# Two gather stages entered by token tile: head 0 of tile 0 is multiplied and searched before tile 1 is turned

## The reference, cut to what matters

```python
q = (ht @ w_query).reshape(T, Hh, 2, PEER_HALF).astype(jnp.float32)   # 8 heads, 2 halves of 128
scores = jnp.einsum('thpd,hpkd->thpk', q, sub_keys)                   # 128 keys per half
s_top, i_top = lax.top_k(scores, K)                                   # K = 16
cand = (s_top[:, :, 0, :, None] + s_top[:, :, 1, None, :]).reshape(T, Hh, K * K)
best, pos = lax.top_k(cand, K)
expert_idx = jnp.take_along_axis(cand_idx, pos, axis=-1)
gates = jax.nn.softmax(best, axis=-1)
...
u = expert_u[idx]
a = jax.nn.gelu(jnp.einsum('tkd,td->tk', u, xb)) * g
return jnp.einsum('tk,tkd->td', a, expert_v[idx])
```

## Time and profile before

| | us |
|---|---|
| median of 3 runs | 2307.51 |
| lowest and highest run | 2303.17, 2310.67 |
| profiled execution, span from first to last instruction | 2302.8 |
| profiled execution, whole time | not given by the page |
| TensorE busy | 1980.1 |
| VectorE busy | 1564.0 |
| ScalarE busy | 1017.4 |
| GpSimd busy | 612.8 |

### The profile page before, as it was taken

How to read it: one execution, slowest core, us unless ns; L and a number is a source line. 1 busy time by engine, 2 the same in 40 slices (tenths; PEclk the granted TensorE clock), 3 DMA queues, 4 the chain that set the end, 5 groups by cost and what they waited for, 6 DMA issues and landing times. The chain is left out here.

```text
span 2302.8 us, 23800 instructions
## 1 busy us (share of the span) xinstructions
PE 1980.1 (86%) x8004; PEld 1232.2 (54%) x8004; DVE 1564.0 (68%) x2910; ACT 1017.4 (44%) x2140; POOL 612.8 (27%) x561
## 2 busy tenths in 40 slices
PE   4999889777877788799978988888888878889998
PEld 3986665222322233379867534433433325878987
DVE  7977776766667676578876677666777654465654
ACT  3344344544444444435444454444454434444443
POOL 0000034443444434100003344344444440220000
PEclk9999899999999999999999999999999999999999
DMA  8786599999999999796667999999999995333553
GB/s 312 281 326 217 187 366 421 421 421 421 421 422 417 422 421 418 319 340 225 231 235 284 421 421 422 420 421 421 418 401 422 421 421 200 115 137 130 183 192 137
DMA packets 112571, 761.74 MB, mean 331 GB/s; under 512 B 12864, under 2 KB 13648, under 8 KB 26304
## 3 DMA queue, kind: packets, MB, share of 16 engines
q0 software_dynamic: 76656, 549.47, 57.6%
q1 hardware_dynamic: 34832, 207.73, 24.3%
q10 hardware_dynamic: 960, 3.01, 0.4%
HBM read 759.12 MB, written 1.05 MB: 330 GB/s over the span
## 5 line engine op out<-in xcount | busy, mean ns | idle before, releaser
L907 PE MATMUL pair<-uv,p_diag 128*128 128x512 f32 x1536 | 761.5, 631 | 190.7 <-ACT p_diag L2117 189.9
L1523 DVE CUSTOM_DVE_ANT_0 uv<-uv,p_h 128x1024 f32<-128x1024 f32 x384 | 470.3, 1225 | 336.8 <-DMA uv<-in_peer_uv,p_idx 336.3
L525 POOL DMA_INDIRECT uv<-in_peer_uv,p_idx x384 | 433.1, 1128 | 737.4 <-PE pair L907 590.0
L907 PEld LDWEIGHTS pair<-uv,p_diag 128*128 128x128 f32 x1536 | 279.1, 195 | 647.9 <-ACT p_diag L2117 391.9
L1172 DVE TENSOR_TENSOR ring_low<-ring,ring_high 128x2048 fp32r<-128x2048 f32 x148 | 336.7, 2287 | 120.3 <-ACT ring_high L1925 119.3
L2111 ACT ACTIVATE p_act<-p_dot 128x1 f32<-128x1 f32 x512 | 103.5, 202 | 652.0 <-DVE p_dot L1523 649.8
L1925 ACT ACTIVATE ring_high<-ring 128x2048 fp32r<-128x2048 f32 x148 | 279.5, 1908 | 182.4 <-DMA ring<-in_ret_w_in 45.5
L672 PE MATMUL pair<-hT_high,ring_high 128*128 128x256 f32 x992 | 287.6, 290 | 3.9 <-DVE hT_low L1182 1.5
L672 PE MATMUL pair<-hT_low,ring_high 128*128 128x256 f32 x992 | 281.9, 284 | 0.0
L672 PE MATMUL pair<-hT_high,ring_low 128*128 128x256 f32 x992 | 281.8, 284 | 0.0
L907 PE MATMUL pair<-uv_high,p_diag 128*128 128x512 f32 x512 | 246.9, 615 | 37.2 <-ACT p_diag L2117 37.1
(11 more groups left out here) (353 smaller groups left out, 2316.6 us busy)
## 6 DMA issues: line engine op xcount, KB each, us to landing
ada<-in_ada_w SPq DMA_DIRECT2D x50, 512.0 KB, 5.8
ring<-in_ret_w_in SPq DMA_DIRECT2D x24, 1024.0 KB, 5.1
ring<-in_sgu_w_in SPq DMA_DIRECT2D x24, 1024.0 KB, 8.1
ring<-in_peer_w_query SPq DMA_DIRECT2D x16, 1024.0 KB, 4.9
ring<-in_w_up SPq DMA_DIRECT2D x16, 1024.0 KB, 4.8
ring<-in_w_down SPq DMA_DIRECT2D x16, 1024.0 KB, 4.8
mod<-in_ada_w SPq DMA_DIRECT2D x30, 512.0 KB, 6.0
ring<-in_sgu_w_out SPq DMA_DIRECT2D x12, 1024.0 KB, 5.4
```

Of the source, the lines that this page charges most:

```text
L525: nc.gpsimd.indirect_dma_start(uv_rows[SLOT[l][s]].rearrange("p a d -> p (a d)"), None, experts, bass.IndirectOffsetOnAxis(ap=p_idx[:, k:k ...
L907: mm = nc.tensor.matmul(acc[:, half, :], p_diag[:, n % DIAGS, :], v[:, half * 512:(half + 1) * 512], start=(k == 0), stop=(k == PICKS - 1))
L1523: V.tensor_tensor_reduce(out=u, in0=u, in1=p_h[:, s // PICKS, :], scale=1.0, scalar=0.0, op0=ALU.mult, op1=ALU.add, accum_out=p_dot[:, n % ...
```

## The change

In both expert layers:

- TensorE turns tile 0 and multiplies head 0 for tile 0 alone (`head_columns(0, (0,))`: 48 matmuls of 128 columns), makes its scores, and only then turns tile 1. Then it multiplies head 1 for both tiles and its scores, and after these head 0 for tile 1 (48 matmuls of 128 columns), with which q0 and q1 become free, and its scores. Head 0 of the chunk has three score groups in place of two.
- Query chunk 1 is no longer multiplied ahead of the picks. Half chunks now stand ahead of picks 0, 2, 8, 14, 20 and 26, scores ahead of 4, 18 and 32. The splits of blocks q4 to q7 and the copies by ScalarE move with them. Blocks q2 and q3 use the two lower places of the high ring too, so pick 5 waits no longer for chunk 1.
- The row of modulation 7 is multiplied ahead of pick 36 (first layer).
- VectorE makes the low half of q0 ahead of tile 0's `finish_tile`, and that of q1 and tile 0's hT lows behind it. Tile 1's hT lows stand behind step 2 of the first search. Lows of q2 and q3 follow the search.
- In the second layer the norm of the memory rows moves from ahead of the picks to pick 22.
- PSUM pairs are numbered by a second order, `PAIR`.

```diff
+QUERY_AT = (0, 2, 8, 14, 20, 26)
+SCORES_AT = (4, 18, 32)
...
+def pairs_in_order():
+
+    out = list(sums_in_order())
+    for l in range(2):
+        i = out.index(("query", l, 0))
+        q0, q1, q2, q3, tile0, tile1, then = out[i:i + 7]
+        out[i:i + 7] = [q0, q1, tile0, q2, q3, then, tile1]
+    return numbered(out)
...
-        out += hT[:2] + (mods(7) if l == 0 else []) + hT[2:]
-        out += [("scores", l, c, t) for c in range(4) for t in range(TT)]
+        out += hT[:2] + [("scores", l, 0, 0)] + hT[2:] + [("scores", l, 0, 1), ("scores", l, 0, 2)]
+        out += [("scores", l, c, t) for c in range(1, 4) for t in range(TT)]
...
-    paired = {i for l in range(2) for i in range(query_first[l] + 4, query_first[l] + 10)} | set(range(kv_first, kv_first + 10))
+    paired = {i for l in range(2) for i in range(query_first[l] + 2, query_first[l] + 10)} | set(range(kv_first, kv_first + 10))
...
                     if s == 5:
-                        pool.wait_ge(sum_ready, SUM[("query", l, 1)] + 1)
+                        pool.wait_ge(sum_ready, SUM[("ret_out" if l == 0 else "sgu_out", 1)] + 1)
...
# TensorE, peer
-                head_product(l, 0)
-                head_scores(l, 0)
-                head_product(l, 1)
-                head_scores(l, 1)
-                columns_product(("query", l, 1), ("query", l), 1, hT)
-                scores(1)
+                turn_rows(n, p_h, (0,))
+                open_sum(("query", l, 0))
+                head_columns(0, (0,)).then_inc(head_ready, 1)
+                pe.wait_ge(keys_in, 16 * (l + 1))
+                pe.wait_ge(head_taken, 2 * l + 1)
+                head_scores(0, 0, (0,))
+                turn_rows(n, p_h, (1,))
+                head_columns(1, (0, 1)).then_inc(head_ready, 1)
+                pe.wait_ge(head_taken, 2 * l + 2)
+                head_scores(1, 1, (0, 1))
+                head_columns(0, (1,), taken=True).then_inc(sum_ready, 1)
+                pe.wait_ge(*taken_sum(("query", l, 0)))
+                head_scores(2, 0, (1,))
...
-                    if s in (2, 10, 18, 26):
-                        part = (2, 10, 18, 26).index(s)
-                        c = 2 + part // 2
+                    if s in QUERY_AT:
+                        part = QUERY_AT.index(s)
+                        c = 1 + part // 2
                         columns_product(("query", l, c), ("query", l), c, hT, parts=(part % 2,))
-                    if s in (16, 32):
-                        scores(1 + s // 16)
-                    if l == 1 and s == 36:
-                        sum_mod(11)
+                    if s in SCORES_AT:
+                        scores(1 + SCORES_AT.index(s))
+                    if s == 36:
+                        sum_mod(7 if l == 0 else 11)
...
# VectorE, finish_tile and last_product_and_norm
-                if n in (1, 3) and t == 1:
-                    lows_hT(n, ((0, 0), (0, 1)))
...
+                    if t == 0:
+                        lows(query_first[n // 2])
                     finish_tile(n, t, h, shift)
-                    lows(query_first[n // 2] + t)
+                    if t == 0:
+                        lows(query_first[n // 2] + 1)
+                        lows_hT(n, ((0, 0), (0, 1)))
...
# VectorE, peer
-                lows_hT(n, ((1, 0), (1, 1)))
                 first = query_first[l]
-                lows(first + 3)
                 for step in range(STEPS):
                     choose(l, 0, step)
+                    if step == 2:
+                        lows_hT(n, ((1, 0), (1, 1)))
                 if l == 1:
-                    norm(6, m_h, m_h, m_row_gain)
-                lows(first + 4)
+                    dve.wait_ge(mem_in, 16)
+                    dve.sem_inc(x_ready, TT)
+                lows(first + 3)
...
-                        if s in (3, 9, 17):
-                            lows(first + 5 + (3, 9, 17).index(s))
+                        if s in (5, 7, 11, 17):
+                            lows(first + 4 + (5, 7, 11, 17).index(s))
+                        if l == 1 and s == 22:
+                            norm(6, m_h, m_h, m_row_gain, begun=True)
...
# ScalarE, peer
+                act.wait_ge(head_ready, 2 * l + 1)
+                take_head(0, (0,), (head_taken, 2 * l + 1))
+                take_head_scores(0, 0, (0,))
+                take_hT(n, ((1, 0), (1, 1)))
+                act.wait_ge(head_ready, 2 * l + 2)
+                take_head(1, (0, 1), (head_taken, 2 * l + 2))
+                take_head_scores(1, 1, (0, 1))
+                exponentials(0)
+                act.wait_ge(sum_ready, SUM[("query", l, 0)] + 1)
+                take_head(0, (1,), taken_sum(("query", l, 0)))
                 highs(first + 3)
...
+                take_head_scores(2, 0, (1,))
                 if l == 1:
                     norm_root(6, m_h)
-                highs(first + 4)
-                take_query(1)
-                take_scores(1)
...
-                        if s in (2, 8, 14):
-                            highs(first + 5 + s // 6)
-                        if s in (13, 29):
-                            take_query(2 + s // 29)
-                        if s in (18, 34):
-                            take_scores(2 + s // 34)
+                        if s in (4, 6, 10, 16):
+                            highs(first + 4 + (4, 6, 10, 16).index(s))
+                        if s in (3, 17, 29):
+                            take_query(1 + (3, 17, 29).index(s))
+                        if s in (5, 20, 34):
+                            take_scores(1 + (5, 20, 34).index(s))
```

More of the change, by code:

```diff
@@ L191, in two_blocks @@
     SUM = sums_in_order()
+    PAIR = pairs_in_order()
     SMALL = small_in_order()
@@ L402, in sum_of @@
         def sum_of(name):
-            return pair[SUM[name] % 3]
+            return pair[PAIR[name] % 3]
         def small_of(name):
             return small[SMALL[name] % 2]
-        kv_pair = (SUM[("peer", 1, 1)] + 1) % 3
+        kv_pair = PAIR[("query", 1, 3)] % 3
         landed = {}
@@ L827, in head_product, with head_scores @@
                                 for j, (a, b) in enumerate(((high, hT[0]), (high, hT[1]), (low, hT[0]))):
[L828 removed]
+                                    mm = nc.tensor.matmul(sum_of(("query", l, 0))[:, head, nt % 2 * S + lo:nt % 2 * S + hi], a[:, k, n_tile], b[:, kk, lo:hi],
                                                           start=(kk == 0 and nt % 2 == 0 and j == 0), stop=(kk == KD - 1 and j == 2),
                                                           skip_group_check=True)
[L831 removed]
+                        if taken and kb == 0:
                             mm.then_inc(w_used, 1)
[L833 to L839 removed]
+                    return mm
+                def head_scores(part_of_chunk, head, tiles):
+                    name = ("scores", l, 0, part_of_chunk)
                     open_small(name)
[L841 to L842 removed]
+                    for q in range(2 * len(tiles)):
+                        t, part = tiles[q // 2], q % 2
                         mm = nc.tensor.matmul(small_of(name)[:, q * P:(q + 1) * P], p_qT[:, 0, 2 * head + part, t * P:(t + 1) * P],
@@ L917, in memory_block @@
                     wait_hT(6)
-                    last = max(i for i in SUM.values() if i < SUM[("peer", 1, 0)] and i % 3 == kv_pair)
-                    pe.wait_ge(sum_taken[kv_pair], last // 3 + 1)
+                    pe.wait_ge(*taken_sum(("query", 1, 3)))
                 if c and kb == 0:
@@ L1466, in choose @@
                 if step == 0:
-                    dve.wait_ge(*taken_small(("scores", l, h // 2, t if h > 1 else h)))
+                    dve.wait_ge(*taken_small(("scores", l, h // 2, t if h > 1 else 1 if h else 2 * t)))
                     for p in range(2):
```

54 lines of the change are left out of this document (16 added, 38 removed).

## The result

The changed kernel takes 2318.0 us (median of 4 runs, 2315.28 to 2318.79), the kernel before 2305.3 in the same session: a ratio of 1.0049, 95% interval 1.0035 to 1.0062. Forecast was 2303.0 with a range of 2297 to 2319, so the time lies inside the range, and the direction was wrong: 0.5% slower where 0.2% faster was forecast. (The forecast was counted from 2307.5, the median of the three runs of before that it had; the same step of 4.5 us from 2305.3 would be 2300.8.) The profiled execution took 2315.28 us with a span of 2313.5.

A forecast was written before the change was run, and what follows sets the result against it. Each gather stage was taken as bound by its bytes at about 421 GB/s. Gains of 4.3 and 1.7 us less 1.4 for holes took 4.6 off a 2302.8 span; with 4.7 between span and median, 2303.0, range 2297 to 2319.

The forecast's parts named there:

- Head 0, tile 0: First stage's entry: 48 matmuls of 128 columns at 0.111 us each; the search starts at 275.8, 9.9 us earlier.
- rival (a): Head 0's narrow matmuls cost as fp32, 0.222 us each, in both stages; total 2320, chance 0.17.
- 5.3 us, from 268.6: First stage: time and start of head 0's 48 narrow matmuls for tile 0, taken at 0.111 us each.
- The clock in the second stage: Second entry: the clock falls to half as before, costing head 0 1.75 us; the search starts at 1210.2.
- Comes back after some 3.5 us of work: Second entry: the fallen clock is full again after some 3.5 us of TensorE work, half of it, 1.75 us, lost.
- Rival (b): The clock falls in the new gaps before head 1 too, both stages, adding 4.5 us to the chain; 2312, chance 0.15.
- The rest of the entry: First stage, search to first gather: index ready at 290.6, 6.6 us earlier; q4 issued at 288.8, 0.85 us later.
- the wait for exp: Entry: VectorE's wait for exp, which stands behind head 1's copy, grows from 1.6 to about 3.6 us.
- The holes: Between the picks, TensorE's cover of the stream is gone: a hole of 0.7 us per stage, bounds 0 and 3.
- 88 against 87: Picks 2 through 32: TensorE has 88 us of work, the stream 87 us of gathers and ring blocks.
- The sum: Whole kernel: gains of 4.3 and 1.7 us less 1.4 for two holes, 4.6 us off, giving 2303.0.

The follow-up runs named there:

- fill: The changed kernel with three fp32 matmuls of 512 columns added on TensorE in its pause ahead of head 0; 2302.5 us, ratio 0.9991.
- exp_first: The changed kernel with the exp put ahead of head 1's copy in ScalarE's queue; 2319.2 us, ratio 1.0064.
- fill_exp: fill with the exp put ahead of head 1's copy in ScalarE's queue, products not spread; 2303.7 us, ratio 0.9993.
- wide: The changed kernel with head 0 of tile 0 multiplied over all 256 columns instead of 128; 2306.5 us, ratio 1.0007.

## Why the prediction was wrong

*Head 0, tile 0: right at one clock, wrong at the other.* 0.111 us per narrow matmul is what they take at 2.4 GHz (267.84 on in fill, and the first 2 us in the changed kernel), so rival (a) is excluded. The Trainium skill (TensorE: Matmul & The Clock Gate, Back-to-back issue gap) gives about 81 ns for a weight load and matmul at 128 columns; that does not come up here at either clock. What failed is the term "5.3 us, from 268.6": I had given stage 1 no fall of the clock at all, though the profile of before has one there, from 270 to 277. The copy came at 277.93 instead of 274.2, the search at 280.1 instead of 275.8.

*The clock in the second stage.* "Comes back after some 3.5 us of work" was read in the profile of before around rows 12, where the clock rose 3.2 us after the first matmul of 256 columns. For 256 columns it is nearly right: wherever head 0, head 1 or chunk 1 began at half clock with 256 columns, they had 2.4 GHz 2.9 to 5.4 us after their first matmul. For the 128 columns of head 0 behind the pause it does not hold: 17 us at half, through head 0, tile 1's turning and part of head 1, where I had 1.75 us lost and 7.5 were, up to 36 us behind the reciprocal. Rival (b) was the nearest in mechanism, with the clock falling in new gaps; it put the fall at head 1 and took 4.5 us for it, and gave 2312.

*The rest of the entry.* With the clock up (fill) it was right in stage 1: the search starts 11.95 us after the reciprocal (forecast 11.75), the wait for exp is 3.91 (3.6), the first gather follows at 27.06 (26.85), and q4 is issued at 24.93 (24.75). In the second stage of fill the first gather goes out at 1225.29, where I had 1225.3, but that is luck, two errors that cancel: the search starts at 1208.70 instead of 1210.2, and the wait for exp is 5.40 instead of 3.6, because the clock is at half for 3.4 us of head 1. This is what rival (b) describes; it came in 8 of the 12 entries of the six kernels with the filler. In the changed kernel the wait for exp was 3.92 in stage 1, where head 1 ran at full clock, and 5.51 in stage 2, where head 1, ahead of the exp in ScalarE's queue, began at half.

*The holes: mis-sized.* 0.7 us per stage were 4.6 and 1.1, and with the clock up still 4.3 and 0.4 ((420-390)/420 x 60, (421-418)/421 x 60). Fill shows it without the clock: its first gathers come 6.4 and 5.1 us sooner after the reciprocal than before (forecast 6.6 and 5.2), and its stretch from the first gather to the 33rd is 6.2 and 4.4 us longer (forecast 3.0 and 4.2), so that stage 1 gains 0.1 us where I had 3.6. The sum "88 against 87" was near the truth, but I let it begin with both sides level. TensorE comes to it late. Its longest waits in the changed kernel between 262 and 400 us (total, times, longest) are one for a pick and one for q2's low half:

```profile
PE pair L919 <- ACT p_diag L2138: 3.7, 1, 3.7
PE pair L685 <- DVE ring_low L1183: 3.5, 1, 3.5
```

I had named the queue of q2's split nowhere; its buffer became that of q0. And I took the index for what begins a stage: exp_first and fill_exp moved it by 4 us and gained nothing. The way to the 33rd gather was TensorE's to set.

*The sum.* Without the clock's fall over head 0 the change with its fillers is at 2302.5, where 2303.0 was forecast, by errors that cancel in part and from another base (2305.3 in place of 2307.5): from the entry's first reciprocal to the exit's first the two stages of fill take 1430.2 us together, against 1434.0 and 1431.5 in the two profiles of before, a gain of 1.3 to 3.8 where I had 4.6. The clock then costs 11 to 15 us (wide, fill). The ways to the 33rd gather show 7.4 to 11.7 us of that; the rest lies behind them, in the stretches that scatter. That 2318.0 is inside the range is luck: the range went up to 2319 for rival (a), which did not happen.

## What to carry to other kernels

When a product is split to start earlier, its pieces are narrower, and behind a pause TensorE's clock may fall over them even though the engine counts as busy. Read the granted clock, and the pause ahead, over matmuls of the same width before taking a price at full clock, and look at what the change takes out of that pause: here it was the row of modulation 7 in stage 1 (the entry by tile with that row left in place was not run). An earlier first transfer was worth nothing here while the engine that frees the buffers had no room in the stretch behind it (exp_first, fill_exp): compare its work there with the stream's, and start the sum with the idle time that the change puts ahead of it. Here three or six small filler matmuls, the exp first and query products spread over more picks turn a loss of 0.5% into a gain of 0.3% (2299.9 and 2299.2 against 2305).

## What the runs showed of the hardware

Behind the same pause of 2.19 us, 48 fp32r matmuls of 128 columns ran at 1.2 GHz for the most part, at a busy share of 1.00, in 16 entries of 16; 48 of 256 columns kept 2.4 GHz in one entry and had it back after 3.4 us in the other. Without such a pause, behind the fillers or behind head 1, the matmuls of 128 columns kept 2.4 GHz. The Trainium skill (TensorE: Matmul & The Clock Gate, the part on the clock gate) has it that activity releases the throttle. Behind the pause the engine was busy without a break over the narrow matmuls, and the throttle was not released before the last of them; the measurement decides.

A narrow matmul with its weight load starts 0.111 us after the last at 2.4 GHz and 0.213 at 1.2. One of 256 columns starts 0.120 us after the last at 2.4 GHz and 0.213 at 1.2 (1209.13 on in before). Half the columns thus saved 8% of a matmul's time at full clock and nothing at half clock: dividing head 0 by tile nearly doubles its work.

In the second profile of the changed kernel the clock was at half from 268 to 288 instead of 271 to 281, and its first gather came at 298.34 us instead of 295.19: the same code is hit differently from run to run.
